# Output phase of a decoder layer: token sums made one by one between the combines, in-place sums made in the sample-memory stage, the second pair's sums ahead of the gate weights'

## What is computed

```python
yb = attend_fn(...).astype(x.dtype) * jax.nn.silu(parts['b_z'])
merged = jax.nn.sigmoid(parts['g_a']) * (ya @ w_a_proj) + jax.nn.sigmoid(parts['g_b']) * (yb @ w_b_proj)
x = x + rmsnorm(merged @ w_out, norm_post)
x = x + (pe @ w_ple) * jax.nn.sigmoid(x @ w_ple_gate)
```

## Time and profile before

| | us |
|---|---|
| three runs | 4181.05, 4180.5, 4182.75 |
| median | 4181.05 |
| profiled execution, its own time | 4183.62 |
| its span, from the first to the last instruction | 4182.0 |

### The profile page before, as it was taken

How to read it: one execution, slowest core, us unless ns; L and a number is a source line. 1 busy time by engine, 2 the same in 40 slices (tenths; PEclk the granted TensorE clock), 3 DMA queues, 4 the chain that set the end, 5 groups by cost and what they waited for, 6 DMA issues and landing times. The chain is left out here.

```text
span 4182.0 us, 41712 instructions
## 1 busy us (share of the span) xinstructions
PE 3957.9 (95%) x14638; PEld 2331.1 (56%) x14638; DVE 2921.3 (70%) x3892; ACT 1416.8 (34%) x2589; POOL 1526.4 (36%) x1420
## 2 busy tenths in 40 slices
PE   6899999999999999999998799899998899989999
PEld 4455555564446655565565466545553788854444
DVE  3579999829999999999996455454444666643333
ACT  3411211153343343333431566555553222111111
POOL 0000036432265666655654222122202755541211
PEclk9999999999999999999999899999998999999999
DMA  5311213330111111111111634222223755531111
GB/s 210 79 61 54 73 59 93 120 118 33 51 42 68 61 68 61 67 67 65 66 67 49 179 111 103 61 88 72 62 92 93 212 154 152 162 139 38 61 56 44
DMA packets 293063, 367.34 MB, mean 88 GB/s; under 512 B 72607, under 2 KB 219571, under 8 KB 290166
## 3 DMA queue, kind: packets, MB, share of 16 engines
q1 hardware_dynamic: 253034, 249.50, 19.8%
q0 software_dynamic: 18704, 85.56, 5.5%
q10 hardware_dynamic: 21120, 29.66, 2.3%
HBM read 235.11 MB, written 128.23 MB: 87 GB/s over the span
## 5 line engine op out<-in xcount | busy, mean ns | idle before, releaser
L1137 DVE MAX8 best<-score 128x8 f32<-128x2048 f32 (+13 forms) x448 | 639.6, 1428 | 15.1 <-POOL score L1102 0.2
L1139 DVE MATCH_REPLACE8 score<-best,score 128x2048 f32<-128x2048 f32 (+13 forms) x448 | 631.1, 1409 | 0.0
L965 PE MATMUL pr<-xnT,w_row 128*128 128x347 f32 (+1 forms) x960 | 297.3, 456 | 0.0
L383 PE MATMUL pg<-xnT,wt 128*128 128x416 f32 x800 | 284.6, 519 | 7.7 <-ACT kT L552 7.7
L1065 POOL TENSOR_TENSOR kT<-kT 128x347 f32<-128x347 f32 (+1 forms) x240 | 194.4, 810 | 230.8 <-ACT kT L1025 224.8
L1503 PE MATMUL mix_slot<-mix_kT,mix_bq 128*128 128x512 f32 (+3 forms) x640 | 271.4, 540 | 4.9 <-DVE mix_mx L1782 4.0
L1558 PE MATMUL mix_po<-mix_probT,mix_v 128*128 128x512 f32 x544 | 240.3, 595 | 1.5 <-ACT mix_probT L1656 1.2
L965 PEld LDWEIGHTS pr<-xnT,w_row 128*128 128x128 f32 x960 | 180.1, 189 | 106.8 <-ACT kT L1025 10.3
L1025 ACT COPY kT<-pr 128x347 f32<-128x347 f32 (+1 forms) x240 | 107.6, 448 | 371.3 <-PE pr L965 365.5
L383 PEld LDWEIGHTS pg<-xnT,wt 128*128 128x128 f32 x800 | 153.8, 193 | 137.2 <-issue 137.0
L1782 DVE CUSTOM_DVE_ANT_0 early<-mix_slot,mix_mk 128x1024 f32<-128x1024 f32 (+7 forms) x86 | 84.8, 986 | 192.7 <-PE mix_pg L1512 143.5
(11 more groups left out here) (613 smaller groups left out, 8038.8 us busy)
## 6 DMA issues: line engine op xcount, KB each, us to landing
gt_scr<-kT SPq DMA_DIRECT2D x40, 694.0 KB, 3.3
out_gm<-gt_scr ACTq DMA_DIRECT2D x32, 520.0 KB
gt_scr<-kT SPq DMA_DIRECT2D x20, 692.0 KB, 4.2
w0a<-in_w_in SPq DMA_DIRECT2D x12, 1024.0 KB, 5.2
wt<-in_w_in SPq DMA_DIRECT2D x22, 512.0 KB, 4.0
w_row<-in_w_in SPq DMA_DIRECT2D x10, 1024.0 KB
qt_scr<-kT POOLq DMA_DIRECT2D x8, 1040.0 KB, 4.2
early<-ybt_scr SPq DMA_DIRECT2D x4, 2080.0 KB, 9.4
```

What stands on the lines that cost most here:

```text
L383: ins = nc.tensor.matmul(pg[0:m, g, 0:GW], w[:, k, 0:m], c["xnT"][:, k, g * GW:(g + 1) * GW], start=k == 0, stop=k == KT - 1)
L965: ins = nc.tensor.matmul(pr[:, b, 0:w], lhs, rhs, start=k == 0, stop=k == 3)
L1137: nc.vector.max(best[:, :], sc).then_inc(top_step, 1)
L1139: nc.vector.match_replace(sc, best[:, :], sc, TAKEN).then_inc(top_step, 1)
```

## The change

Seven edits:

1. `terms` is cut into four parts, at k = 21, 22, 23 and 24, each behind the combine of its product on DVE. The in-place sum comes first; the sum in `t[:, 0]` is now made from `t[:, 1]` and `b11`.
2. PE waits for each sum at the product that reads it: weight sums at j = 1, 3 and 5, token sums at j = 1, 2 and 6.
3. The in-place sums of branch B's four weight column pairs and of the first pass's tokens are made by POOL at the end of the sample-memory stage; `weight_sums` makes them no more for branch B, and at the start of the output phase DVE makes three token sums instead of four.
4. In that stage the gate rows `zb` get four rooms instead of one; SP loads them right behind `yb`, and POOL makes all four first products, then all four second ones.
5. `out_sums(1)` is made right behind `out_sums(0)`, ahead of the gate weights' sums, into `sg` instead of `so`.
6. `gate_sums(0)` therefore waits until PE has made product j = 5 of O 1.
7. In the entries of the second part, product j = 5 of O 1 comes ahead of the transposes X 0 instead of behind them.

The diff, cut to its core:

```diff
@@ -2393,7 +2393,7 @@
-def sample_memory_phase(nc, c, d, inputs, early):
+def sample_memory_phase(nc, c, d, inputs, first, early):
@@ -2424,7 +2424,8 @@
-        yb, zb = first_operands(early)
+        yb, zb0 = first_operands(early)
+        zb = [zb0] + [sb(f"zb{x}", [P, ZK, TW])[:, :, :] for x in range(1, QUARTERS)]
@@ -2441,26 +2442,27 @@
-        yb_loaded, zb_loaded, z_mult, z_sig, yb_ready = (sem(n) for n in ("yb_loaded", "zb_loaded", "z_mult", "z_sig", "yb_ready"))
+        yb_loaded, z_mult, z_sig, yb_ready = (sem(n) for n in ("yb_loaded", "z_mult", "z_sig", "yb_ready"))
+        zb_loaded = [sem(f"zb_loaded{x}") for x in range(QUARTERS)]
+        first_sums = sem("first_sums")
+        w1, wb_loaded = first
...
         def _(sp):
             def load_zb(x):
-                if x:
-                    sp.wait_ge(yb_ready, x)
...
-                sp.dma_start(zb, d["gt"][lo:lo + ZK, :, 0:TW].rearrange("k p s -> p k s")).then_inc(zb_loaded, 16)
+                sp.dma_start(zb[x], d["gt"][lo:lo + ZK, :, 0:TW].rearrange("k p s -> p k s")).then_inc(zb_loaded[x], 16)
...
+            for x in range(1, QUARTERS):
+                load_zb(x)
...
             for hh in range(AH):
-                if hh + 1 < QUARTERS:
-                    load_zb(hh + 1)
@@ -2485,11 +2487,21 @@
             for x in range(QUARTERS):
...
-                pool.wait_ge(zb_loaded, 16 * (x + 1))
-                nc.gpsimd.tensor_tensor(y, y, zb, ALU.mult).then_inc(z_mult, 1)
+                pool.wait_ge(zb_loaded[x], 16)
+                nc.gpsimd.tensor_tensor(y, y, zb[x], ALU.mult).then_inc(z_mult, 1)
+            for x in range(QUARTERS):
+                y = yb[:, ZK * x:ZK * x + ZK, :]
...
-                nc.gpsimd.tensor_tensor(y, y, zb, ALU.mult).then_inc(yb_ready, 1)
+                nc.gpsimd.tensor_tensor(y, y, zb[x], ALU.mult).then_inc(yb_ready, 1)
+            pool.wait_ge(wb_loaded, 16)
+            for pair in range(COLUMN_PAIRS):
+                lo = 2 * P * pair
+                nc.gpsimd.tensor_tensor(w1[:, 0:4, lo + P:lo + 2 * P], w1[:, 0:4, lo:lo + P], w1[:, 0:4, lo + P:lo + 2 * P], ALU.subtract
+                                        ).then_inc(first_sums, 1)
+            pool.wait_ge(yb_ready, QUARTERS)
+            nc.gpsimd.tensor_tensor(yb[:, 0:4, TG:TW], yb[:, 0:4, TG:TW], yb[:, 0:4, 0:TG], ALU.subtract).then_inc(first_sums, 1)
+            pool.wait_ge(first_sums, COLUMN_PAIRS + 1)
...
         def _(dve):
@@ -2609,7 +2621,7 @@
             def gate(x):
...
-                nc.scalar.activation(zb, zb, ACT.Sigmoid).then_inc(z_sig, 1)
+                nc.scalar.activation(zb[x], zb[x], ACT.Sigmoid).then_inc(z_sig, 1)
@@ -2762,7 +2774,7 @@
-    events = [("wsum", 0), ("terms", 0, 0)]
+    events = [("wsum", 0)] + [("terms", 0, 0, part) for part in (1, 2, 3)]
@@ -2773,13 +2785,13 @@
             if not branch:
...
-                if k == 21:
-                    events.append(("terms", g, 1))
+                if 21 <= k <= 24:
+                    events.append(("terms", g, 1, k - 21))
             elif g + 1 < PASSES:
...
-                if k == 21:
-                    events.append(("terms", g + 1, 0))
+                if 21 <= k <= 24:
+                    events.append(("terms", g + 1, 0, k - 21))
             elif k in tw_at:
@@ -2804,7 +2816,7 @@
         if q == 0:
-            entries += o[0:5] + turn + o[5:7] + rows
+            entries += o[0:6] + turn + o[6:7] + rows
@@ -2887,6 +2899,7 @@
+        out_terms = [so, sg] + [so] * (PAIRS - 2)
@@ -2926,7 +2939,11 @@
         def weight_sums_done(u):
...
-            return SUMS * (u + 1) + sum(unit_of(x)[0] == 0 for x in range(u + 1))
+            return SUMS * (u + 1) + sum(unit_of(x)[0:2] == (0, 1) for x in range(u + 1))
...
+        def terms_done(g, branch):
...
+            return 4 * (2 * g + branch + 1) - 1
@@ -3065,11 +3082,13 @@
             def out_sums(q):
...
-                if q:
+                if q > 2:
...
-                sums(mt[q % 2], so, so_step, q)
+                sums(mt[q % 2], out_terms[q], so_step, q)
...
             def gate_sums(q):
+                if q == 0:
+                    pool.wait_ge(entry_mm, done("O", 1, 5))
@@ -3085,13 +3104,11 @@
-                if u == 0:
-                    pool.wait_ge(wb_loaded, 16)
...
-                if g == 0:
+                if branch and g == 0:
@@ -3108,6 +3125,7 @@
+                    out_sums(1)
@@ -3116,7 +3134,6 @@
-            out_sums(1)
...
             def store(q):
@@ -3155,16 +3172,14 @@
-                    if e == 0 and j == 0:
-                        pe.wait_ge(wb_loaded, 16)
...
-                    if j == 1:
-                        pe.wait_ge(s_step, weight_sums_done(e))
-                        if pair == 0:
-                            pe.wait_ge(t_step, 4 * (2 * g + branch + 1))
+                    if j in (1, 3, 5):
+                        pe.wait_ge(s_step, weight_sums_done(e) - 2 + j // 2)
+                    if pair == 0 and j in (1, 2, 6):
+                        pe.wait_ge(t_step, terms_done(g, branch) - (2 if j == 1 else 1 if j == 2 else 0))
@@ -3213,7 +3228,7 @@
                         if q == 0:
...
-                    ins = winograd(v, j, mt[q % 2], so, w1, tw)
+                    ins = winograd(v, j, mt[q % 2], out_terms[q], w1, tw)
@@ -3427,20 +3442,25 @@
-            def terms(g, branch):
+            def terms(g, branch, part):
...
-                t, base = token_sums[branch], 4 * (2 * g + branch)
-                if branch:
-                    dve.wait_ge(yT_ready, 2 * PIECES * (g + 1))
-                elif g:
-                    dve.wait_ge(yb_ready, QUARTERS * g)
-                nc.vector.tensor_tensor(t[:, 0, :, :], b22, b12, ALU.subtract).then_inc(t_step, 1)
-                dve.wait_ge(t_step, base + 1)
-                nc.vector.tensor_tensor(b12, b12, b11, ALU.subtract).then_inc(t_step, 1)
-                dve.wait_ge(t_step, base + 2)
-                nc.vector.tensor_tensor(t[:, 1, :, :], b22, b12, ALU.subtract).then_inc(t_step, 1)
-                dve.wait_ge(t_step, base + 3)
-                nc.vector.tensor_tensor(t[:, 2, :, :], t[:, 1, :, :], b21, ALU.subtract).then_inc(t_step, 1)
+                t, base = token_sums[branch], terms_done(g, branch) - 3
+                if part == 0:
+                    if branch:
+                        dve.wait_ge(yT_ready, 2 * PIECES * (g + 1))
+                    else:
+                        dve.wait_ge(yb_ready, QUARTERS * g)
+                    nc.vector.tensor_tensor(b12, b12, b11, ALU.subtract).then_inc(t_step, 1)
+                elif part == 1:
+                    if g or branch:
+                        dve.wait_ge(t_step, base)
+                    nc.vector.tensor_tensor(t[:, 1, :, :], b22, b12, ALU.subtract).then_inc(t_step, 1)
+                elif part == 2:
+                    dve.wait_ge(t_step, base + 1)
+                    nc.vector.tensor_tensor(t[:, 0, :, :], t[:, 1, :, :], b11, ALU.subtract).then_inc(t_step, 1)
+                else:
+                    dve.wait_ge(t_step, base + 1)
+                    nc.vector.tensor_tensor(t[:, 2, :, :], t[:, 1, :, :], b21, ALU.subtract).then_inc(t_step, 1)
@@ -3610,7 +3630,7 @@
-            sample_memory_phase(nc, c, d, inputs, early)
+            sample_memory_phase(nc, c, d, inputs, first, early)
```

## The result

The kernel before: 4182.51 us, median of six runs (4180.5 to 4195.86). The changed kernel: 4165.65 us, median of six (4152.6 to 4171.41). The comparison gives a ratio of 0.9936 (95% interval 0.9914 to 0.9957), 27 us faster; the two medians alone give 17. I had forecast 4146 us, a ratio of 0.9916, with a range of 4137 to 4159: the direction is right, the gain came out at two thirds of the forecast, and the median of the six runs lies 6.7 us above my range. Carried by its ratio to the 4181.05 us that the forecast starts from, the time is 4154 us, inside it.

The account below looks back on a forecast made before the run. TensorE, busy 95% of the span, bounds the kernel; its waits and the slow clock behind them can be won. Terms 5.5 - 27 - 13.6 = -35.1 us take 4183.62 to 4148.5; the median lies 2.6 lower, 4146 us, range 4137 to 4159.

Parts of the forecast that it names:

- Token sums, -27: Seven branch or pass boundaries of the output phase: 19.0 us of combine waits plus 9.1 of slow products go, less 1.1.
- my upper end: Token sums at the seven boundaries: the largest gain given, -28.1 us; the smallest was -13.
- the replay's margins: Boundaries replayed with sums at 2.2 us: combine 1 ready at 3411.8, wanted at 3414.8; combine 4 at 3420.0, wanted 3420.1.
- DVE stays late: Rival, 0.17: at the boundaries combines and sums together run past PE, short waits remain, about 13 of 27 us stay: 4159.
- Second pair, -13.6: Second part of the output phase: waits of 10.4 and 1.1 us and a slow product go, less 0.7; ends -14.3 and -6.
- The feared late combine: Second pair's sums on POOL lengthen two of DVE's output-weight sums beside them: 0 to 2 us, taken at 0.7.
- First sums, tail of the memory stage, +6.3: Sums behind POOL's last gate product end at 3244.6, so the output phase starts at about 3246.8, 6.3 us later.
- Its return of 0.8 us within the phase: Start of the output phase: net cost +5.5 us, less the 6.3 by which the phase starts later, makes -0.8.
- Run beside DVE's small operations (0 to 1 us, taken as 0): Sample-memory stage: with gate rows loaded sooner, POOL's gate products run beside small VectorE operations, at no cost.
- one slow product, 1.8 us: Clock cost behind a TensorE wait: two products at a boundary took 5.30 us where 3.51 is normal, 1.79 lost.
- forecast -41.4: Output-phase terms together: -27 for token sums, -13.6 for the second pair, -0.8 for the phase's start.
- The start costs little: Rival, 0.14: gate rows land earlier because the memory stage's stores have drained; the start is near +1, time 4141.

Follow-up runs that it names:

- half sums: The changed kernel with each of the four in-place weight sums at the end of the memory stage split into two halves; 4158.5 us, ratio 0.9934.
- products in a row: The changed kernel without in-place sums in the memory stage (made in the output phase), its four first gate products still consecutive; 4165.1 us, ratio 0.9927.

## Why the prediction was right and where it failed

- **Token sums, -27:** right in mechanism, 2 us too small. 30.1 us of output phase for this part alone, 0.9 of them the start's and 29.2 the seven places'; my upper end was 28.1. None of the seven combines is late, and the replay's margins were real; the rival "DVE stays late" did not happen.
- **Second pair, -13.6:** right, 13.1 between two profiles. The feared late combine came to 0.94 us.
- **First sums, tail of the memory stage, +6.3:** right by itself. From the start of the last gate product to the output phase it is 11.8 us instead of 5.8, +5.9. And TensorE did not keep what it bought, as I said: the waits of the phase's start went to 2.14 us for ScalarE, 1.35 for a combine and 3.18 behind the gate rows, with a slow product behind it. Its return of 0.8 us within the phase did not come (0.2 us lost instead).
- **"Run beside DVE's small operations (0 to 1 us, taken as 0)":** this step failed. I looked at the length of VectorE's operations and not at their number or at who waits for them. Eight scalings met two of the products that GpSimd now makes in a row; they took 2.5 us more, and TensorE waited for what comes behind them. With 1.0 us for the half-speed update behind that wait, the profile has +9.4 instead of +6.3.
- **The clock behind it:** I priced a wait of TensorE with one slow product, 1.8 us, as in the earlier trace rows. Ahead of the state loop a wait can be followed by half speed for most of the loop. A slow loop is worth 17 to 21 us (four profiles), and 3.2 us of added scalings, with a wait of 3.75 us, cost 26 us by median. The change's wait there grew from 0.48 to 2.98 us. Whether that makes the 10 to 13 us between its medians and the profiled execution is not shown and stays open: its second profile has 4.8 us of it in the loop (53.6 us), but "half sums", with a wait of 3.03 us, had a median only 2 us above its profiled execution, and in "products in a row" the profiled execution was at half speed before the loop began, with no wait there.
- **Sum:** in the profile -42.2 (forecast -41.4), +9.4 (+6.3), and 1.8 lost ahead of the scalings. In the runs some 22 to 27 us by the ratios instead of 35.
- **"The start costs little" (0.14)** did not occur; what would have been cheap was to leave the sums where they were.

## What to carry to other kernels

Before moving work to an engine that "idles", lay its instructions beside those of the engine it takes turns with, one by one: many short instructions on a path that someone waits for can each lose a whole partner instruction (1.28 us for a scaling of 0.28), so the count matters, not the busy share. Where a dependence is relaxed (here a wait per product), price the other parts of a change again after it; the part in the memory stage bought nothing once the waits were split. And a new wait of TensorE ahead of a stretch that it paces can cost more than its length: here 3.3 us of it went with 26 us of median. The chance of that shows only in several runs, and one profiled execution can fall on either side.

## What the hardware showed that I had not expected

- One scaling of VectorE (32x256, 0.28 us alone) takes the length of one GpSimd instruction: 1.28 us beside sums of 1.27, 0.74 beside halves of 0.71.
- TensorE's granted clock in a loop of 120 matmul records, busy for some nine tenths of it: 0.87 or 0.55 to 0.60 in different executions of the same or nearly the same code, 47.9 or 65 to 69 us. The Trainium skill, TensorE: Matmul & The Clock Gate, "What's actually happening", says that idling lowers the clock, that activity raises it, and that the point varies between runs. The fall behind 3.75 us agrees with that. That the clock then stays at half for most of a loop in which TensorE is 90% busy does not, and here the measurement decides. Why it stays down, and why in some executions only, was not tried and stays open.
